# Depthwise-convolution taps over all 512 tokens at once instead of two halves of 256, with the normalized rows kept in the accumulator's room

## The reference

```python
def conv_mixer(u, w_dw, b_dw, ln_g, ln_b):
    a, gate = jnp.split(u, 2, axis=-1)
    h = a * jax.nn.sigmoid(gate)
    h = lax.conv_general_dilated(
        h, w_dw[:, None, :].astype(h.dtype), window_strides=(1,),
        padding=[(CONV_WIDTH - 1, 0)],
...
        feature_group_count=GROUP) + b_dw
    hf = h.astype(jnp.float32)
    mu = jnp.mean(hf, axis=-1, keepdims=True)
    var = jnp.mean(jnp.square(hf - mu), axis=-1, keepdims=True)
    hf = (hf - mu) * lax.rsqrt(var + 1e-5) * ln_g + ln_b
    return jax.nn.silu(hf).astype(u.dtype)
...
for l in range(DEPTH):
    h = rms_norm(x, attn_pre_g[l])
    u = jnp.einsum('bsd,de->bse', h, w_in[l])
...
    y = jnp.concatenate([y_a, y_b, y_c, y_d], axis=-1)
    y = jnp.einsum('bse,ed->bsd', y, w_out[l])
    x = x + rms_norm(y, attn_post_g[l])
    h = rms_norm(x, ffn_pre_g[l])
    f = jax.nn.silu(jnp.einsum('bsd,df->bsf', h, w_gate[l])) * jnp.einsum('bsd,df->bsf', h, w_up[l])
    f = jnp.einsum('bsf,fd->bsd', f, w_down[l])
    x = x + rms_norm(f, ffn_post_g[l])
```

## Time and profile before

| what | us |
|---|---|
| median of 3 runs (lowest to highest) | 1108.68 (1108.66 to 1112.82) |
| the profiled execution: time | 1109.05 |
| its span, first to last instruction | 1107.2 |
| TensorE busy | 1079.1 |
| VectorE busy | 620.5 |
| ScalarE busy | 410.3 |

### The profile page before, as it was taken

How to read it: one execution, slowest core, us unless ns; L and a number is a source line. 1 busy time by engine, 2 the same in 40 slices (tenths; PEclk the granted TensorE clock), 3 DMA queues, 4 the chain that set the end, 5 groups by cost and what they waited for, 6 DMA issues and landing times.

```text
span 1107.2 us, 16624 instructions
## 1 busy us (share of the span) xinstructions
PE 1079.1 (97%) x6640; PEld 656.5 (59%) x6640; DVE 620.5 (56%) x1418; ACT 410.3 (37%) x810; POOL 5.1 (0%) x18
## 2 busy tenths in 40 slices
PE   5999999999999999999999999999999999999997
PEld 4888785596444444444478878747844444444443
DVE  5898998884324324312568989889624324322014
ACT  4454635454323323212234463455523323322001
POOL 1000000000000000000000000000000000000000
PEclk9999999999999999999999999999999999999999
DMA  7442403155234233233003341034533333232001
GB/s 272 132 131 77 154 1 115 39 177 164 80 113 149 80 114 112 95 99 114 1 1 115 115 135 57 1 114 135 176 110 110 101 113 111 81 113 76 1 20 57
DMA packets 58172, 109.64 MB, mean 99 GB/s; under 512 B 7024, under 2 KB 7280, under 8 KB 57968
## 3 DMA queue, kind: packets, MB, share of 16 engines
q1 hardware_dynamic: 58096, 108.58, 31.1%
HBM read 106.46 MB, written 2.10 MB: 98 GB/s over the span
## 4 chain that ended last, share of the span: by engine, by line
PE 88%; DVE 6%; DMA 4%; issue 1%; ACT 1%; SPq 0%; ACTq 0%; DVEq 0%
PE ps L493 82%; DMA raw<-weights_dram 3%; PE ps L497 3%; DVE ring L1134 2%; DVE E L1255 2%; PE ps L696 1%; PE ps L680 1%; DMA gbc<-gains_dram 1%; DVE E L1207 0%; ACT ring L758 0%; DVE small L1437 0%; DVE hT L1215 0%; ACT gbc L758 0%; DVE U L1358 0%; PE ps L657 0%
## 5 line engine op out<-in xcount | busy, mean ns | idle before, releaser
L493 PE MATMUL ps<-hT,ring 128*128 128x512 f16 (+1 forms) x3264 | 549.0, 330 | 2.8 <-DVE hT L1215 2.7
L493 PEld LDWEIGHTS ps<-hT,ring 128*128 128x128 f16 x3264 | 320.4, 98 | 226.6 <-issue 3.1
L493 PE MATMUL ps<-ring,U 128*128 128x512 f16 x1440 | 313.4, 379 | 0.0
L1134 DVE SCALAR_TENSOR_TENSOR ring<-raw,ring 128x512 f16<-128x512 f32 x376 | 236.8, 685 | 97.5 <-ACT ring L758 96.7
L758 ACT ACTIVATE ring<-raw 128x512 f16<-128x512 f32 x376 | 212.9, 622 | 140.3 <-PE ps L493 81.2
L493 PEld LDWEIGHTS ps<-ring,U 128*128 128x128 f16 x1440 | 140.8, 98 | 167.1 <-issue 0.3
L1458 DVE SCALAR_TENSOR_TENSOR R<-ps,R 128x512 f32<-128x512 f32 (+1 forms) x52 | 31.7, 609 | 255.4 <-ACT R L933 255.0
L493 PE MATMUL ps<-ring,hT 128*128 128x256 f16 x1152 | 134.3, 273 | 0.0
L933 ACT ACTIVATE R<-ps 128x512 f32<-128x512 f32 (+1 forms) x52 | 27.5, 530 | 275.4 <-PE ps L493 275.4
L493 PEld LDWEIGHTS ps<-ring,hT 128*128 128x128 f16 x1152 | 112.2, 98 | 14.2 <-issue 1.1
L1255 DVE SCALAR_TENSOR_TENSOR E<-E,par 128x256 f32<-128x256 f32 x240 | 101.7, 477 | 0.2
(11 more groups left out here) (104 smaller groups left out, 475.7 us busy)
## 6 DMA issues: line engine op xcount, KB each, us to landing
raw<-weights_dram SPq DMA_DIRECT2D x376, 256.0 KB, 3.4
gbc<-gains_dram SPq DMA_DIRECT2D x8, 512.0 KB, 6.1
xs<-x_dram SPq DMA_DIRECT2D x4, 512.0 KB, 5.3
out_dram<-xs SPq DMA_DIRECT2D x8, 256.0 KB, 2.0
cst<-consts_dram SPq DMA_DIRECT2D x1, 1296.0 KB, 8.2
bd<-pool_w_dram SPq DMA_DIRECT2D x8, 16.0 KB, 5.6
par<-params_dram SPq DMA_DIRECT2D x1, 76.0 KB, 6.0
cst<-consts_dram SPq DMA_DIRECT2D x1, 64.0 KB, 5.8
```

The costliest lines, as they stand in the source:

```text
L493: ins = mm(dst, st, mv_, start=first and i == 0, stop=last and i == 2, **kw)
L1134: V.scalar_tensor_tensor(out=ring[:, slot % RING, 1, raw_part(part)], in0=raw[:, n % NRAW, :], scalar=W_SCALE, in1=ring[:, slot % RING, 0, ...
```

## The change

Four things change together.

1. `conv(l, n)` runs each tap over 512 tokens, so a layer has 62 taps in place of 124. It waits for both halves of `glu`. `conv_sb` counts once a layer, and both `conv_T` wait for the same last tap.
2. `cacc` is twice as wide. The separate buffer `cn` for the normalized rows is gone; they are written over the accumulator columns of their own half. `conv_scale` on ScalarE loses one wait. The array `E` keeps its 4672 columns.
3. No taps fill the short chains of `conv_norm` and `ret_norm` any more.
4. The call lists of VectorE and ScalarE and the ticks in `AT` are new throughout.

```diff
-        (rz_w, cn_w, yb_w, m1, m2, hb_w, ca_w, mo_w) = carve(
-            E, [2 * HALF, 2 * G, 2 * HALF, 2 * HALF, 2 * HALF, 2 * (CW - 1 + S), 2 * HALF, 2 * G])
+        (rz_w, yb_w, m1, m2, hb_w, ca_w, mo_w) = carve(
+            E, [2 * HALF, 2 * HALF, 2 * HALF, 2 * HALF, 2 * (CW - 1 + S), 2 * S, 2 * G])
...
+        cn = [cacc[:, :, HALF * s:HALF * (s + 1)] for s in range(2)]
...
             def conv_T(l, s):
-                pe.wait_ge(conv_sb, hs(l, s))
+                pe.wait_ge(conv_sb, l + 1)
                 take(5, convN_sb, 2 * hs(l, s))
                 for t in range(2):
                     for c in range(2):
-                        last = transpose(b256(5)[:, t, P * c:P * (c + 1)], cacc[:, c, tok(t)])
+                        last = transpose(b256(5)[:, t, P * c:P * (c + 1)], cacc[:, c, tok(2 * s + t)])
...
             def conv_scale(l, s):
                 act.wait_ge(conv_rs, hs(l, s))
-                if hs(l, s) > 1:
-                    act.wait_ge(convY_ps, hs(l, s) - 1)
...
-            def conv(l, s, n):
-
-                if (l, s) not in taps_done:
-                    taps_done[(l, s)] = 0
-                    dve.wait_ge(hb_sb, hs(l, s))
-                    if hs(l, s) > 1:
-                        dve.wait_ge(convT_ps, hs(l, s) - 1)
-                    if s == 0:
+            def conv(l, n):
+
+                if l not in taps_done:
+                    taps_done[l] = 0
+                    dve.wait_ge(hb_sb, hs(l, 1))
+                    if l:
+                        dve.wait_ge(convY_ps, hs(l - 1, 1))
+                    else:
                         dve.wait_ge(hT_ps, xno("pre", l, NT - 1) + 1)
...
-                    src = hbuf[:, c, HALF * s + k:HALF * s + k + HALF]
+                    src = hbuf[:, c, k:k + S]
...
-        ("pre_T", 2): 55, ("pre_T", 3): 57, ("moba_T", 0): 101, ("moba_T", 1): 115, ("moba_stage", 0): 121,
+        ("pre_T", 2): 50, ("pre_T", 3): 53, ("moba_T", 0): 104, ("moba_T", 1): 142, ("moba_stage", 0): 151,
```

More of the change, by code:

```diff
@@ L131 @@
-        ("pre_T", 1): 970,
-    },
-    {
[L134 to L143, removed]
+        ("pre_T", 2): 50, ("pre_T", 3): 53, ("moba_T", 0): 104, ("moba_T", 1): 142, ("moba_stage", 0): 151,
@@ new lines @@
+        ("moba_stage", 1): 163, ("moba_T", 2): 178, ("moba_stage", 2): 179, ("moba_stage", 3): 190,
+        ("moba_T", 3): 209, ("moba_stage", 4): 212, ("moba_stage", 5): 215, ("moba_stage", 6): 218,
+        ("moba_Y", 0): 228, ("conv_T", 0): 234, ("moba_stage", 7): 256, ("ret_T", 0): 260, ("conv_Y", 0): 260,
+        ("ret_S", 0): 262, ("ret_O", 0): 267, ("ret_T", 1): 267, ("moba_stage", 8): 268, ("ret_S", 1): 271,
+        ("ret_O", 1): 272, ("moba_stage", 9): 272, ("moba_stage", 10): 287, ("moba_stage", 11): 288,
@@ new lines @@
+        ("ret_T", 2): 289, ("moba_Y", 1): 292, ("ret_S", 2): 299, ("ret_Y", 0): 304, ("pool_Y", 0): 305,
+        ("ret_T", 3): 306, ("ret_O", 2): 306, ("ret_S", 3): 308, ("ret_O", 3): 313, ("conv_T", 1): 315,
+        ("conv_Y", 1): 328, ("ret_Y", 1): 344, ("pool_Y", 1): 345, ("fpre_T", 0): 362, ("fpre_T", 1): 374,
+        ("fpre_T", 2): 436, ("fpre_T", 3): 436, ("pre_T", 0): 955, ("pre_T", 1): 964,
+    },
+    {
+        ("pre_T", 2): 29, ("pre_T", 3): 36, ("moba_T", 0): 102, ("moba_T", 1): 123, ("moba_stage", 0): 125,
+        ("moba_stage", 1): 166, ("moba_T", 2): 174, ("moba_stage", 2): 178, ("moba_stage", 3): 195,
+        ("moba_T", 3): 205, ("moba_stage", 4): 209, ("moba_stage", 5): 219, ("moba_stage", 6): 221,
+        ("moba_Y", 0): 225, ("conv_T", 0): 236, ("moba_stage", 7): 257, ("ret_T", 0): 258, ("conv_Y", 0): 260,
+        ("ret_S", 0): 263, ("ret_O", 0): 266, ("ret_T", 1): 267, ("moba_stage", 8): 268, ("ret_S", 1): 270,
+        ("ret_O", 1): 271, ("moba_stage", 9): 272, ("moba_stage", 10): 281, ("moba_stage", 11): 282,
+        ("ret_T", 2): 288, ("ret_S", 2): 291, ("moba_Y", 1): 294, ("ret_T", 3): 304, ("ret_Y", 0): 304,
+        ("pool_Y", 0): 304, ("ret_O", 2): 305, ("ret_S", 3): 308, ("ret_O", 3): 312, ("conv_T", 1): 316,
+        ("conv_Y", 1): 329, ("ret_Y", 1): 341, ("pool_Y", 1): 346, ("fpre_T", 0): 367, ("fpre_T", 1): 374,
+        ("fpre_T", 2): 436, ("fpre_T", 3): 440, ("pre_T", 0): 948, ("pre_T", 1): 964,
@@ L144 @@
     },
 ]
+E_COLS = 7 * 2 * HALF + 2 * (CW - 1 + S) + 4
 PAR = {}
@@ L1546, in _ @@
-                split_lo(z + 10)
-                conv_norm(l, 0, lambda: conv(l, 1, 1))
-                conv(l, 1, 1)
-                m_max(l, 2, 0)
-                m_max(l, 2, 1)
-                ret_rotate(l, 0, 1)
+                conv(l, 13)
+                m_norm(l, 1)
+                m_max(l, 2, 0)
+                conv(l, 4)
+                lo_of(b256(5), moba_hi, 4, l, 0, A_SCALE, moba_y)
+                m_max(l, 2, 1)
+                conv(l, 2 * CW)
+                split_lo(z + 9)
@@ L1552, in _ @@
+                conv_norm(l, 0)
+                zero(l)
                 m_max(l, 2, 2)
                 m_max(l, 2, 3)
-                split_lo(z + 11)
-                conv(l, 1, 2)
+                split_lo(z + 10)
                 ret_mask(l, 0)
                 conv_out(l, 0)
-                split_lo(z + 12)
                 ret_state(l, 0)
-                conv(l, 1, 4)
+                split_lo(z + 11)
                 m_max(l, 3, 0)
                 m_max(l, 3, 1)
-                split_lo(z + 13)
@@ L1564, in _ @@
-                conv(l, 1, 1)
                 lo_of(ybuf, conv_hi, 0, l, 0, 0.5 * A_SCALE, conv_y)
                 ret_mask(l, 1)
-                split_lo(z + 14)
+                split_lo(z + 12)
                 ret_state(l, 1)
```

199 lines of the change are left out of this document (91 added, 108 removed).

## The result

The changed kernel takes 1113.24 us (median of 20 runs, 1111.54 to 1116.1); the kernel before, run beside it, takes 1110.82 (20 runs, 1107.87 to 1117.26). The ratio is 1.0022, with a 95% interval of 1.0012 to 1.0032: slower by about 2.4 us, which is within the 0.5% that the prediction called the least difference to tell. The profiled execution is one of the slower ones: 1114.66 us, 5.6 above the profiled execution of before. So 3 us of what follows from the two traces belongs to that execution and not to the kernel's median.

What follows compares the result with a forecast made beforehand. TensorE, busy 1079.1 of 1107.2 us, was taken as the bound. 1109.05 + 1.7 + 0.7 + 1.0 - 1.9 = 1110.55 profiled, less 0.37 to the median: 1110.2 us, range 1105 to 1115, chance 0.80 within 0.5%.

Steps and rivals of the forecast that it cites:

- VectorE's time was not the price: Whole kernel: 16 us less VectorE time buy little; at most 7.7 us of TensorE's idle time can be reached.
- The tap: VectorE's convolution: a wide tap takes 0.745 us, starting 0.664 after the last; 8 us saved a layer, 16 in all.
- The opening of layer 0: Up to half 1: new order of splits, `h_lo_of` and `glu` makes TensorE start at 44.4, not 42.68: +1.7 us (1.0 to 2.4).
- TensorE is the bound from there to the end, so it is not given back: From layer 0's half 1 to the end: the opening's +1.7 us stays in the total.
- Ahead of `conv_T(0)`: Layer 0, ticks 228 to 234: TensorE waits 0.7 us for the last tap behind `moba_Y(0)`; bounds 0 and 2, both layers.
- masks: `ret_O(1)` three products behind `ret_S(1)`: TensorE waits 0.5 us in both layers, +1.0; bounds 0.6 and 2.
- the 1.10: Layer 0, at 163.38: TensorE's 1.10 us wait for a retention mask goes, part of the -1.9.
- layer 1's 0.52: Layer 1: `conv_T(1)`'s 0.5 us wait for the last tap of half 1 goes, part of the -1.9.
- the third rival: Stages 7 to 11, moved to ticks 256 to 288 among retention tiles: ten more waits of 0.65 us, 1116.7; chance 0.04.
- The freed time: First rival, mixer windows: freed VectorE time drains TensorE's waits, at most 7.7 us, to 1101.0; chance 0.07.
- The late join: Second rival, tick 234: dearer wide taps make both convolution halves late, 1114 to 1117.5, said 1116; chance 0.09.
- the attention copies' waits: Mixers: TensorE's 4.1 us of waits for ScalarE's attention copies; half going was only in the -4 bound.

Runs made afterwards that it cites:

- b_fewtaps: Kernel before with 60 of a layer's 124 narrow taps left out (convolution not computed in full): 1108.54 us, ratio 0.9989.
- a_again: The changed kernel unedited, run and profiled a second time: 1114.51 us, ratio 1.0028 to the kernel before.
- a_shift_gaps: `a_shift` with layer 0's `conv_T(0)` three ticks later and two more ticks between `ret_S(1)` and `ret_O(1)`: 1115.19 us, ratio 1.0048 to the kernel before.
- a_open2: Changed kernel with the opening of before: `glu`, both `h_lo_of` and ScalarE's copies ahead of slot 4's splits, ticks 55 and 57: 1117.21 us, ratio 1.0050.
- a_shift: `a_open2` with both maxima of stage 0 behind 18 of the layer's taps, where they stood behind 22 and 26: 1114.4 us, ratio 1.0040 to the kernel before.
- b_again: The kernel before, unedited, run and profiled a second time: 1110.63 us, ratio 0.9999.
- a_few: `a_open2` with 30 of a layer's 62 wide taps left out (convolution not computed in full): 1111.55 us, ratio 1.0005 to the kernel before.
- a_narrow: Changed kernel's order with each wide tap issued as two taps of 256 columns: 1126.53 us, ratio 1.0147 to the kernel before.
- a_open: Changed kernel with slot 4's splits behind the token tiles' copies but `glu` still behind the splits, ticks 55 and 57: 1116.36 us, ratio 1.0047.
- b_open: Kernel before with the changed kernel's order and ticks up to the start of half 1, narrow taps kept: 1112.16 us, ratio 1.0004.

## Why the prediction was right, and where it was not

**The forecast, no change that can be told, held.** It set the changed kernel 1.5 us above the kernel before (1110.55 against 1109.05, profile to profile); the medians lie 2.4 apart. The predicted 1110.2 is 3.0 below the measured 1113.24, and 2.1 of that is the level: the three runs shown had a median of 1108.68, twenty have 1110.82.

**VectorE's time was not the price: right for the order before.** `b_fewtaps` shows it: three times the saving buys less than 3 us.

**The tap: right.** 743 ns and 0.663 apart, forecast 745 and 0.664. The busy time was mis-stated: 89 us was 120 durations laid end to end, while the group counts overlaps once and shows 81.4. VectorE's whole saving is 13.4 us; the prediction gave 16, less a part for the chains. The section of the Trainium skill that it cites ("VectorE: DVE Perf Modes", "The DRAIN you can't avoid") says in the same place that an operation that is not held starts earlier, and the wide taps agree: 0.663 apart at 743 ns each.

**The opening of layer 0: the order right, the size off.** The term was +1.7, half 1 at 44.4; the profile has 47.40, 3.0 later. By its rows 1.81 are slot 3's split, which came late in that execution (32.65 against 30.84); 0.33 a wait in front of `norm_x`; 0.87 the wait for ScalarE's splits at 41.98, behind transposes at the lower clock. At an equal arrival of slot 3 the order costs 2.8 (`a_again` against `a_shift_gaps`), so the term was 1.1 short. The prediction priced no fall of the clock, since the earlier trace rows show none before the last window: here TensorE stood idle for 2.36 us, the clock fell, and it cost 1.5. The Trainium skill ("TensorE: Matmul & The Clock Gate", part 1, "The HAM clock gate") has the two levels and a fall after idling; the trace agrees, with 0.58 over 38.4 to 42.0 behind the 2.36 us.

**"TensorE is the bound from there to the end, so it is not given back": this step failed.** In layer 0 of the changed kernel VectorE's chain sets the time of attention stage 1, or is within 0.7 us of it. The second maximum comes at 80.3 to 80.6 with or without the late opening, and `a_open2`, whose half 1 starts 4.75 us sooner, pays 1.20 and 2.47 us in waits and a fall of the clock instead. The +1.7 and the loss at stage 1 are not two terms; the later of the two counts. The walk through the places where something new is close skipped stage 1: it took the first maximum as one "which TensorE sets at about tick 151" and counted the taps from there to the join at tick 234, where it found slack, and not those ahead of it, right behind the second `glu`. A wide tap cannot start before that `glu`, which waits behind the splits of slots 5 to 7 for their transfers until 59.4 to 60.3. With half 1 started on time, 5.8 of VectorE's 18 us before it stay empty (2.2 in the kernel before, whose second `glu` came no sooner, at 62.48, but where narrow taps of half 0 stood in the gaps), and the taps that weren't done then are in front of stage 1. That the maxima are this wait's cause is shown by `a_shift`; that most of what VectorE saves in layer 0 is spent in this way is argued from the windows.

**The small terms: right.** Ahead of `conv_T(0)` 0.57 (forecast 0.7); masks 0.41 twice (0.5 twice); the 1.10 and layer 1's 0.52 gone. From the start of half 1 to tick 320, layer 0 takes 127.4 us in place of 127.9 (47.40 to 174.78, 42.68 to 170.58). The sum forecast -0.2 there. But `a_shift_gaps` shows what such a term is not: a price that a later tick would save.

**Layer 1: a term was missing.** Its mixers, from their first product to tick 320, take 150.3 us in place of 148.9 (`a_again` 149.8, `b_again` 148.8): +1.0 to +1.4, where the sum had the masks' +0.5 and -0.5 for the tap, so nothing. TensorE's timeline, layer 1 of the changed kernel:

```profile
667.26 0.63 PE L498 MATMUL ps<-cst,R 128*128 128x128 f32 x4 [0.63 <-ACT gbc L906]
...
674.99 0.52 PE L498 MATMUL ps<-cst,gbc 128*128 128x128 f32 x3 [0.83 <-ACT U L759]
...
679.83 0.72 PE L601 MATMUL ps<-R 64*128 64x128 f32 x8 [0.31 <-issue]
681.40 0.66 PE L616 MATMUL ps<-U,R 128*128 128x64 f32 x4 [0.41 <-DVE R L1346]
```

These are waits of the stages that moved to ticks 256 to 288, the third rival's place, at a small part of its price. `a_few` has the stretch at 150.5 us with half the taps left out, so it is not VectorE's taps. It lies in the new ticks and ScalarE's order; which of the two was not tried.

**The rivals.** The freed time did not drain the waits. The late join did not come about, since the pitch was 0.663; `a_narrow` shows what lay behind it. (The prediction calls a pitch equal to the duration the third rival's case; it is the second's.)

**How much of it was luck.** The direction was forecast, and the total is within 0.9 us of the forecast difference. But the opening was 1.1 us short, layer 1 lacked 1.0 to 1.4, and half of the attention copies' waits went, which stood in the bounds and not in the sum. A forecast of no change within 0.5% hides errors of this size.

**Open.** Slot 3's split came at 32.6 to 33.1 in the changed kernel, `a_again` and `a_narrow`, and at 29.9 to 30.1 in `a_open` and `a_open2`, which do not differ from it up to there. Four kernels with one and the same opening have 29.85 (`a_few`), 29.88 (`a_open2`), 30.58 (`a_shift`) and 33.06 (`a_shift_gaps`). In `b_open` it came at 31.4, in both profiles of before at 30.8 to 30.9. So the arrival of weights varies from execution to execution by as much as the changed kernel differs; whether the kernel has a part in it as well, single profiles do not tell. How much of the 2.4 us of the medians is the opening and how much layer 1 is argued from the stretches, not shown by one experiment.

## What to carry to other kernels

Fewer, wider operations save time on their engine, but each starts later, since it needs all of its input; ask what else stands ahead of the last piece of that input (here splits of weights still on their way), what the engine does until then, and count the work that is piled up in front of the first small result that the busiest engine needs, not only in front of the join. A delay ahead of such a point costs nothing if the point is set by the other engine anyway: before a loss is repaired, look whether the next wait stands ready to take the gain. The saved engine time itself should be priced in the order that it is spent in, for which leaving out half of the operations is a quick test.
